# A two-block kernel: latent projections on unscaled rows, head scales spread by DMA, angles computed earlier

## The reference

```python
h = rmsnorm(x, norm_g)
proj = h @ w_in          # q_lat 384, kv_lat 256, k_pe 32, ...
q = (rmsnorm(q_lat, q_norm_g) @ w_uq).reshape(B, S, N_HEADS_MLA, QK_HEAD_DIM)
kv = (rmsnorm(kv_lat, kv_norm_g) @ w_ukv).reshape(B, S, N_HEADS_MLA, QK_NOPE_DIM + V_HEAD_DIM)
k_nope, v = split_cols(kv, (QK_NOPE_DIM, V_HEAD_DIM))
q = rope_tail(rmsnorm(q, q_head_g), cos, sin)
k = rope_tail(rmsnorm(k, k_head_g), cos, sin)
o_attn = blocked_bidirectional_attention(q, k, v) * jax.nn.silu(g_attn)
```

## Time and profile before

| | us |
|---|---|
| median of 3 runs | 2633.99 (2633.96 to 2637.42) |
| the profiled execution, its own time | 2636.41 |
| its span, first to last instruction | 2634.3 |
| PE busy in the span | 2507.5 (95%) |
| DVE, POOL, ACT busy | 1313.3, 873.7, 756.2 |
| from the last MLP matmul to the first matmul of lat | 1303.62 to 1324.52 |
| heads, first matmul to last sums | 1404.67 to 1499.31 |
| first scores of MLA | 1525.53 |

### The profile page before, as it was taken

One profiled execution on the slowest core, in us unless ns is written; L12 is line 12 of the kernel. 1 busy time (PEld: TensorE's weight loads), 2 busy tenths in 40 slices (PEclk: granted clock), 3 DMA queues, 4 the chain that ended last, 5 costly groups with the idle time before them and its releaser, 6 DMA issues.

```text
span 2634.3 us, 33963 instructions
## 1 busy us (share of the span) xinstructions
PE 2507.5 (95%) x13700; PEld 2048.6 (78%) x13700; DVE 1313.3 (50%) x1325; ACT 756.2 (29%) x1158; POOL 873.7 (33%) x383
## 2 busy tenths in 40 slices
PE   6999888899999999999899989999999999989999
PEld 3788677677888888888677678888888878878877
DVE  3799688636444445444575777741023221341341
ACT  4201277614111211111144367731000120241010
POOL 1444300043434444344333200024444434423442
PEclk8999899999999999999999999999999999999999
DMA  6111455211111111111211000011111111113112
GB/s 258 43 45 56 126 171 178 107 55 37 53 48 49 48 48 48 48 48 48 88 56 40 25 1 1 1 33 49 50 63 48 49 41 50 64 40 112 49 48 88
DMA packets 54965, 165.31 MB, mean 63 GB/s; under 512 B 5364, under 2 KB 23928, under 8 KB 53432
## 3 DMA queue, kind: packets, MB, share of 16 engines
q1 hardware_dynamic: 49152, 140.68, 16.2%
q10 hardware_dynamic: 5688, 22.81, 2.2%
HBM read 152.98 MB, written 10.49 MB: 62 GB/s over the span
## 4 chain that ended last, share of the span: by engine, by line
PE 85%; DVE 7%; ACT 3%; issue 2%; POOL 1%; DMA 1%; SPq 0%; DVEq 0%; ACTq 0%; POOLq 0%
PE region L275 25%; PE region L277 24%; PE region L276 24%; PE aux L1789 2%; PE pv L1799 2%; PE pv L369 1%; DVE conv L1139 1%; ACT na_prob L1023 1%; DMA x_sb<-x_t 1%; DVE na_prob L1064 1%; POOL w_hi L2211 1%; POOL w_lo L2214 1%; PE pv L833 1%; PE region L2083 1%; PE pv L983 1%
## 5 line engine op out<-in xcount | busy, mean ns | idle before, releaser
L2211 POOL TENSOR_TENSOR w_hi<-w_raw,der 128x1024 fp32r<-128x1024 f32 x186 | 363.5, 1954 | 1550.6 <-PE region L277 1522.2
L275 PE MATMUL region<-h_hi,w_hi 128*128 128x512 f32 x1760 | 692.2, 393 | 15.0 <-DVE h_lo L440 5.4
L276 PE MATMUL region<-h_lo,w_hi 128*128 128x512 f32 x1760 | 688.1, 391 | 0.0
L277 PE MATMUL region<-h_hi,w_lo 128*128 128x512 f32 x1760 | 687.8, 391 | 0.0
L2214 POOL TENSOR_TENSOR w_lo<-w_raw,w_hi 128x1024 fp32r<-128x1024 f32 x186 | 502.6, 2702 | 14.6
L275 PEld LDWEIGHTS region<-h_hi,w_hi 128*128 128x128 f32 x1760 | 332.4, 189 | 94.3 <-issue 11.9
L277 PEld LDWEIGHTS region<-h_hi,w_lo 128*128 128x128 f32 x1760 | 332.3, 189 | 70.2
L276 PEld LDWEIGHTS region<-h_lo,w_hi 128*128 128x128 f32 x1760 | 332.6, 189 | 68.0
L275 PE MATMUL region<-ff_hi,w_hi 128*128 128x512 f32 x512 | 199.2, 389 | 0.0
L276 PE MATMUL region<-ff_lo,w_hi 128*128 128x512 f32 x512 | 199.2, 389 | 0.0
L277 PE MATMUL region<-ff_hi,w_lo 128*128 128x512 f32 x512 | 199.2, 389 | 0.0
(11 more groups left out here) (351 smaller groups left out, 3764.0 us busy)
## 6 DMA issues: line engine op xcount, KB each, us to landing
w_raw<-units SPq DMA_DIRECT2D x186, 512.0 KB, 3.3
w_raw<-w_ada_late SPq DMA_DIRECT2D x32, 512.0 KB, 4.3
bias<-na_bias SPq DMA_DIRECT2D x24, 384.0 KB, 3.7
ada_buf<-w_ada SPq DMA_DIRECT2D x4, 2048.0 KB, 28.5
x_sb<-x_t ACTq DMA_DIRECT2D x2, 2048.0 KB, 13.7
v_pair<-v_spill SPq DMA_DIRECT2D x64, 64.0 KB, 3.4
x<-x_t ACTq DMA_DIRECT2D x1, 4096.0 KB, 14.8
x_spill<-x ACTq DMA_DIRECT2D x1, 4096.0 KB, 11.2
```

The lines of the kernel that those rows point to most:

```text
L275: pe.matmul(dst, wh, xh, start=first, stop=False)
L276: pe.matmul(dst, wh, xl, start=False, stop=False)
L277: return pe.matmul(dst, wl, xh, start=False, stop=last)
L2211: pool.tensor_tensor(w_hi[:, s], w_raw[:, s], one_col.broadcast_to([P, 1024]), ALU.mult)\
```

## The change

Five things are changed together, all between the MLP and MLA.

1. **Unscaled start of lat.** In the last MLP group ACT and DVE also split `x1` times the gain, without the norm's scale, into `h2_hi` and `h2_lo`. The first two lat units are projected from these; the nf sums stand among their blocks as the sixth, the spread as the eleventh. `n3_act` and `n3_dve` then overwrite the parts with scaled ones for units 3 to 6, each block once unit 2 has used it (`lat_free`), and DVE multiplies the first two results by the scale (`scale`).
2. **Angles earlier.** The angle steps (two for each of the 8 first units) and both sines run in the first MLP group, which is taken out of the loop, as the last is.
3. **Head scales.** `half_ones` packs a head's sums in 8 groups of 16 rows, so root and reciprocal work on 128 columns. PE spreads nothing: SP stores 8 rows of 128 to DRAM, waits for that, and loads the line into all 128 partitions of one of three SBUF tiles (`head_wide0` to `2`). `finish` is two heads late in place of one and reads that tile. The root of head h waits for the load of head h-2.
4. **SP's order.** Six unit loads stand between these pairs of DMAs.
5. **No meeting before MLA**; ACT rounds the first head among the copies of uv.

```diff
             for f in range(KD):
+                if first and f == 6:
+                    sine(0, sin2)
...
             for d in range(KD):
+                if first and d == 1:
+                    sine(1, cos2)
...
+                if last:
+                    e.activation(h2_hi[:, d], x1[:, d], ACT.Identity, scale=both_g[:, d:d + 1]).then_inc(sem("nu_hi"), 1)
+
+        group(0, True, False)
+        with e.Fori(1, FF_GROUPS - 1) as g:
+            group(g, False, False)
+        group(FF_GROUPS - 1, False, True)
...
                     low(f - 1)
+                if first:
+                    angle_dve(e, ch, 2 * f)
+                    angle_dve(e, ch, 2 * f + 1)
...
+                if last:
+                    reach(e, "nu_hi", d + 1)
+                    e.scalar_tensor_tensor(out=h2_lo[:, d], in0=x1[:, d], scalar=both_g[:, d:d + 1], in1=h2_hi[:, d].bitcast(F32),
+                                           op0=ALU.mult, op1=ALU.subtract).then_inc(sem("nu_lo"), 1)
...
-    def nf_pe(e, pos):
+    def nf_sums_pe(e):
         reach(e, "nf_acc", 14 * FF_GROUPS + 1)
         packed_sums(e, aux[:, 0:QTR], tmp[:, 2]).then_inc(sem("nf_sqmm"), 1)
         packed_sums(e, aux[:, HALF:HALF + QTR], tmp[:, 3]).then_inc(sem("nf_sqmm"), 1)
+
+    def nf_spread_pe(e):
         reach(e, "nf_rs", 1)
         spread(e, pv_flat, nf_b).then_inc(sem("nf_spread"), 1)
...
+    def n3_act(e, pos):
+        for k in range(KD):
+            t = tmp[:, k % 2]
+            reach(e, "n3_nm", k + 1)
+            e.activation(t, t, ACT.Identity, scale=both_g[:, k:k + 1]).then_inc(sem("n3_af"), 1)
+            reach(e, "n3_af", k + 1)
+            if k < KD - 1:
+                reach(e, "lat_free", k + 1)
+            else:
+                e.wait_ge(unit_done, UNIT0["lat"] + 2)
+            copy(e, h2_hi[:, k], t).then_inc(sem("n3_hi"), 1)
+            if k in (2, 3):
+                use = pos.next_use()
+                e.wait_ge(unit_done, UNIT0["lat"] + k - 1)
+                copy(e, q_lat[:, k - 2], region[:, use % 2]).then_inc(free[use % 2], 1)
+
+    def n3_dve(e, pos):
+        def low(k):
+            reach(e, "n3_hi", k + 1)
+            e.tensor_tensor(h2_lo[:, k], tmp[:, k % 2], h2_hi[:, k].bitcast(F32), ALU.subtract).then_inc(sem("n3_lo"), 1)
+
+        def scale(i):
+            use = pos.next_use()
+            e.wait_ge(free[use % 2], use // 2 + 1)
+            e.tensor_tensor(q_lat[:, i], q_lat[:, i], pv_flat, ALU.mult).then_inc(sem("lat_scaled"), 1)
+
+        for k in range(KD):
+            if k >= 2:
+                reach(e, "n3_lo", k - 1)
+            e.tensor_tensor(tmp[:, k % 2], x1[:, k], pv_flat, ALU.mult).then_inc(sem("n3_nm"), 1)
+            if k:
+                low(k - 1)
+        low(KD - 1)
+        scale(0)
+        scale(1)
+        reach(e, "n3_lo", KD)
...
-        start_pair(e, pos, UNIT0["lat"], h2_hi, h2_lo, lambda k: reach(e, "n3_lo", k + 1))
-        unit(2)
-        unit(3)
+        assert pos.use % 2 == 0 and UNIT0["lat"] % 2 == 0
+        for i, (n, k) in enumerate(LAGGED):
+            if i == 5:
+                nf_sums_pe(e)
+            if i == 10:
+                nf_spread_pe(e)
+            if k == 0:
+                e.wait_ge(unit_split, UNIT0["lat"] + n + 1)
+                wait_region(e, pos.use + n)
+            if n == 0:
+                reach(e, "nu_lo", k + 1)
+            w = slice(k * P, k * P + P)
+            for lo in (0, HALF):
+                last = mm3(e, region[:, n, lo:lo + HALF], w_hi[:, n, w], w_lo[:, n, w],
+                           h2_hi[:, k, lo:lo + HALF], h2_lo[:, k, lo:lo + HALF], k == 0, k == KD - 1)
+            if k == KD - 1:
+                last.then_inc(unit_done, 1)
+            elif n == 1:
+                last.then_inc(sem("lat_free"), 1)
+        pos.use += 2
+        start_pair(e, pos, UNIT0["lat"] + 2, h2_hi, h2_lo, lambda k: reach(e, "n3_lo", k + 1))
...
         for i in range(LATS):
-            use = pos.next_use()
-            e.wait_ge(unit_done, UNIT0["lat"] + i + 1)
             dst = q_lat[:, i] if i < NQL else kv_lat[:, i - NQL]
-            copy(e, dst, region[:, use % 2]).then_inc(free[use % 2], 1)
-            e.wait_ge(free[use % 2], use // 2 + 1)
+            if i < 2:
+                reach(e, "lat_scaled", i + 1)
+            else:
+                use = pos.next_use()
+                e.wait_ge(unit_done, UNIT0["lat"] + i + 1)
+                copy(e, dst, region[:, use % 2]).then_inc(free[use % 2], 1)
+                e.wait_ge(free[use % 2], use // 2 + 1)
...
-            if i < 2:
-                reach(e, "angle", i + 1)
-                e.activation((sin2, cos2)[i][RR], tmp[RR, 2], ACT.Sin).then_inc(sem("table"), 1)
...
-        reach(e, "pos_ld", 16)
-        ch(e.tensor_copy(tmp[r, 0], pos_i[r]))
-        ch(e.tensor_scalar(tmp[r, 0], tmp[r, 0], par[r, SMALL["invf"]:SMALL["invf"] + 1], None, ALU.mult))
...
-        for which, (quarter, shift) in enumerate([(0.0, 0.0), (0.25, np.pi / 2)]):
-            ch(e.tensor_scalar(tmp[r, 1], tmp[r, 0], 1.0 / TWO_PI, quarter, ALU.mult, ALU.add))
-            ch(e.tensor_scalar(tmp[r, 1], tmp[r, 1], magic, magic, ALU.add, ALU.subtract))
...
-            e.tensor_scalar(tmp[r, 2], tmp[r, 2], -3.1415925, None, ALU.max).then_inc(sem("angle"), 1)
-        reach(e, "angle", 2)
-        reach(e, "table", 1)
+        reach(e, "table", 2)
         ch(e.tensor_scalar(sin2[r], sin2[r], par[r, SMALL["sign"]:SMALL["sign"] + 1], None, ALU.mult))
-        reach(e, "table", 2)
         ch(e.memset(q_table[0:NOPE], 1.0))
         ch(e.tensor_copy(q_table[NOPE:QK], cos2[NOPE:QK]))
         ch(e.tensor_copy(q_table[QK:P], sin2[QK:P]))
+        ch(e.memset(half_ones[:], 0.0))
+        for a in range(2):
+            ch(e.memset(half_ones[:, a, 16 * a:16 * a + 16], 1.0))
...
+        def __init__(self, tag, heads, scale, wide=None):
+            self.tag, self.heads, self.scale_at, self.wide = tag, heads, scale, wide
+
+        def spread_sp(self, e, h):
+            reach(e, f"{self.tag}_rs", h + 1)
+            if h >= 3:
+                reach(e, f"{self.tag}_sc", h - 2)
+            line = v_spill[0, 8 * h:8 * h + 8]
+            e.dma_start(line, self.scale_at[0:P:16, h % 2, 0:P]).then_inc(sem("wide_st"), 16)
+            reach(e, "wide_st", 16 * (h + 1))
+            e.dma_start(self.wide[h % 3][:], line.rearrange("a c -> (a c)").partition_broadcast(P)).then_inc(sem(f"wide_ld{h % 2}"), 16)
+
+        def reach_wide(self, e, h):
+            reach(e, f"wide_ld{h % 2}", 16 * (h // 2 + 1))
 
...
+                    for a in range(2):
+                        for q in range(4):
+                            at = (2 * q + a) * P
+                            last = e.matmul(aux[32 * q:32 * q + 32, bank:bank + P], half_ones[0:rows, a], src[:, at:at + P],
+                                            start=(a == 0), stop=(a == 1))
+                elif self.heads[h].packed:
                     last = packed_sums(e, aux[:, bank:bank + QTR], src, rows)
                 else:
...
-                if h >= 2:
+                if h >= 2 and not self.wide:
                     spread_scale(h - 2)
             n = len(self.heads)
             sums(n - 1)
-            spread_scale(n - 2)
+            if not self.wide:
+                spread_scale(n - 2)
             if meanwhile:
                 meanwhile()
-            spread_scale(n - 1)
+            if not self.wide:
+                spread_scale(n - 1)
 
...
                 reach(e, f"{tag}_ss", h + 1)
                 if h >= 2:
-                    if self.heads[h - 2].packed:
+                    if self.wide:
+                        self.reach_wide(e, h - 2)
+                    elif self.heads[h - 2].packed:
                         reach(e, f"{tag}_spread", sum(x.packed for x in self.heads[:h - 1]))
                     else:
                         reach(e, f"{tag}_sc", h - 1)
                 bank = (h % 2) * HALF
-                root_act(e, tag, self.scale_at[:, h % 2], aux[:, bank:bank + QTR], self.heads[h].rows, eps_col)
+                n = P if self.wide else QTR
+                root_act(e, tag, self.scale_at[:, h % 2, 0:n], aux[:, bank:bank + n], self.heads[h].rows, eps_col)
 
             for h, head in enumerate(self.heads):
                 use = pos.next_use()
...
+                if self.wide:
+                    self.reach_wide(e, h)
+                elif packed:
                     reach(e, f"{tag}_spread", sum(x.packed for x in self.heads[:h + 1]))
-                rs = pv_flat if packed else self.scale_at[:, h % 2]
+                rs = self.wide[h % 3] if self.wide else pv_flat if packed else self.scale_at[:, h % 2]
                 self.heads[h].finish(e, ch, self.heads[h].dst, rs)
                 e.sem_inc(sem(f"{tag}_sc"), 1)
 
+            late = 2 if self.wide else 1
             for h in range(len(self.heads)):
                 pos.next_use()
-                inverse_dve(e, tag, h + 1, self.scale_at[:, h % 2])
```

(41 more changed lines are left out.)

70 lines of the change are left out of this document (47 added, 23 removed).

## The result

| kernel | median us | runs | against before, 95% interval | span of the profiled run | mean clock |
|---|---|---|---|---|---|
| before | 2634.77 | 2633.96 to 2637.42 | | 2634.3 | |
| after | 2597.89 | 2597.12 to 2600.76 | 0.986 (0.9843 to 0.9877) | 2595.3 | 0.986 |

The change gives 36.9 us by the medians and 39.0 by the spans. The forecast was 44, to 2590, in a range of 2576 to 2606. The start of lat gave 2.5 us more than its term and the heads gave 6.4 us less, so the total came out nearer than its terms. The two stretches of the traces give 17.5 + 22.6 = 40.1 us; the spans have 39.0, because after reached the MLP 0.7 us later and took 0.4 us more behind the first scores.

The account below looks back on a forecast made before the run. PE was taken to bound the heads before the change, DVE's queue beside POOL's splits after it. Part A's 15 us and part B's 29 make 44, from the median 2634.0 to 2590 us; range 2576 to 2606.

Parts of the forecast that it names:

- Part A: Unscaled start of lat behind the MLP: 19.2 us gained at most, less 4 of stall, so 15 us (11 to 19).
- Waits, slow start and spread: PE behind the MLP: three waits of 14.9 us, slow restart 2.4, spread 1.9 would go, together 19.2 us.
- The stall: In lat, PE waits for scaled blocks whose remainders DVE makes late beside POOL's splits: 4 us, 0 and 8 as ends.
- third rival: Lat: scaled blocks come 8 us or more late, ACT copying two results between them; part A gives 4, 2601 us; chance 0.08.
- The collisions: Lat: each of two POOL splits catches about 1.1 of DVE's remainders, 2.2 us each, 5 us late after two.
- The rival of a moved wait: Lat: the unscaled start moves the wait instead of removing it, blocks 8 us or more late; 2601 us, chance 0.08.
- Angles and extra roundings: Moved into the MLP's first group and added in its last, hidden by DVE's idle time: nothing either way.
- Part B: Heads, from their start to the first scores: 120.9 us becomes 92, a gain of 29 us (20 to 39).
- DVE's work: Heads: 5 heads at 5.9 us, 3 at 4.7 and 8 at 4.4, together 79 us.
- the charge for POOL: Heads: 2 us of DVE time for each POOL split, on every second q head and every third k head.
- The round trip: Heads' scales: store 2.0, load 3.3, issue and semaphores 0.8 us; hidden under DVE's 4.4 a head until the last head.
- The slow rival: Heads: the broadcast load takes 17 us, part B 171 us, 50 lost and 15 won, 2669 us; chance 0.05.

Follow-up runs that it names:

- unscaled_alone: The unscaled start of lat and the earlier angles alone, with the heads as in before: 2619.12 us, 0.9938 of before.
- copy_early: after with ACT's two copies of the unscaled first lat results out of PSUM one position earlier in ACT's order: 2595.50 us, 0.9845 of before.
- turn_early: after with DVE's five operations that turn the keys' rotary rows put beside heads 0 and 1 instead of 1 to 5: 2594.03 us, 0.9833 of before.
- turn_after_store: after with the edits of turn_early and root_after_store together: 2593.71 us, 0.9842 of before.
- root_after_store: after with ACT's root of head h waiting for the store of head h-2's scales, not their load: 2597.87 us, 0.9858 of before.
- two_stores: after with each head's scales stored twice, one after the other, to lengthen each round trip: 2612.27 us, 0.9901 of before.

## Why the prediction was right, and where it was off

**Part A, 15 us (11 to 19), was 17.5** (100.66 to 83.14; 18.1 in unscaled_alone). Waits, slow start and spread went as summed: PE goes on without a gap and the clock stays at 1.00 up to the third product. The stall was taken at 4 us and came to about that, 2.25 of gap and 1.7 by eight matmuls at the lower clock behind it; that the number fits is luck. Its cause was another: PE was held by ACT's copy out of PSUM, which the prediction named only in its third rival, and not by the remainders. copy_early showed that the remainders are next in line, with 2.58 us. The collisions were lighter than charged: 2.2 us had been put on each of 2.2 remainders, 4.8 in sum; four were caught (2.26, 2.17, 1.66, 2.17 against 1.22 us), for 0.4 to 1.0 us each, 3.4 in sum. What made the gain larger is that the sums, which were to stay at 1.9 us, took 1.07, and that two waits of 0.40 and 0.34 us later in lat are gone; some 0.7 us stay open. The rival of a moved wait (8 us) did not come. Angles and extra roundings cost nothing, as forecast: the first group of the MLP takes 176.8 us in after and in before, the last 174.2 in both.

**Part B, 29 us (20 to 39), was 22.6** (120.9 to 98.3; 21.0 with both at the slow start, so that 1.6 us of it are the luck of one execution). The mechanism was that of the forecast: DVE's queue and POOL beside it. The terms against the trace:
- DVE's work was put at 79 us. From the heads' start it was 3 reciprocals and one rotation before 1408.5, 3.6 us, and 75.0 us from there to the end of the last finishing (1483.52), with 1.26 of waiting for the last load in it: 77.3 of work. Right, and with it the charge for POOL (12.8 us, where 5 x 1.0, 3 x 1.0 and 8 x 0.7, 13.6 us, had been put on the heads). But "`finish` read PSUM" held for one of its two operations on q only: the multiplication by `q_table` had both inputs in SBUF already, and the rotation too, and they carry 7.0 of the 12.8.
- The start was the failed step: "DVE starts when head 1 is projected and head 0 summed, some 11 us in". Only the reciprocals start there. Finishing 0 stands in DVE's order behind reciprocal 2, since finishing is two heads late now. It started 20.7 us in (1408.55), while its load had landed some 4 us before. DVE had 3.6 us of work until then instead of 9.7: 6.1 us lost on a queue that is full from there on.
- The tail was put at 2.4 us and took 2.6. So 20.7 + 75.0 + 2.6 = 98.3, where 11 + 79 + 2.4 = 92 had been forecast, and the start is nearly the whole of the difference: 20.7 - 11 - 3.6 = 6.1. Of after's start the quick first head took off 1.6 us; in copy_early, with the slow one, finishing 0 starts 22.3 us in.
- The instructions' order, which was known, held this before the run. The sum used DVE's total work with a start time, and not the place of the first long operation in the queue. turn_early and turn_after_store, which put other work into that hole, bear it out with 4.7 and 4.9 us; a kernel that finishes one head late with these loads was not run.

**The round trip**, 6.1 us taken, took 5.1 to 6.5 from a reciprocal's end to what its load releases, median 5.8 over the eleven that were waited for (store to load 1.65 as a rule, load 3.3 to 4.3, median 3.8). The Trainium skill, "DMA: Bandwidth & Descriptors", § Anatomy of one DMA, gives its 2.0 us and 436 GB/s for DMAs that GpSimd issues, and these are issued by SyncE, which the prediction passed over. By it the trip was 5.2 us as an estimate; the runs put the median at 0.6 more. "Under DVE's 4.4, so it is hidden until the last head" holds for after (root_after_store), with little room (two_stores). The slow rival, 17 us for a broadcast load, is out. "SP's six unit loads, nothing" is a bit off. A load issued shortly ahead of a store draws the step from store to load out:

```profile
1441.95 0.32 SPq L1728 DMA_DIRECT2D head_wide<-v_spill  x1
1443.69 0.57 SPq L1726 DMA_DIRECT2D v_spill<-head_scale  x1
1446.04 0.32 SPq L1728 DMA_DIRECT2D head_wide<-v_spill  x1
...
1472.83 0.43 SPq L2282 DMA_DIRECT2D w_raw<-units  x1
1474.49 0.57 SPq L1726 DMA_DIRECT2D v_spill<-head_scale  x1
1477.39 0.32 SPq L1728 DMA_DIRECT2D head_wide<-v_spill  x1
```

2.35 us behind a load of scales, where DVE's queue hides it; 2.90 behind the last unit load, and that is the last trip, for which DVE then waits 1.26 us.

**What the prediction didn't have as a term**: the meeting and the copies of values, 5.3 us, which it counted within part B without a price.

## What to carry to other kernels

When a scale is applied one head later to hide a transfer, the engine that applies it has less to do at the start and the same to do in all; on a full queue, what it didn't do at the start comes back at the end (6.1 us here), so give it the side work in that hole (4.7 us won back). A wait that the profile puts down to a DMA may belong to the engine that feeds the DMA: take the transfer out of the wait and see whether the wait stays. And moving an operand out of PSUM to save an engine's turn makes the reader a neighbour of POOL; count the splits that fall beside it, and beside the operations that had both inputs in SBUF before, since a new order moves them too. Last, two lengths cut from a trace tell more than a median where the edits are worth less than the scatter ahead of the place they touch.

## What the runs showed of the hardware

- In the heads, a DVE operation of 1024 columns with both inputs in SBUF took 1.22 to 1.29 us alone and up to 3.3 beside a POOL split; with the splits cut to 16 columns none was over 1.29. It isn't slowed but held: all 13 such operations of after from 1320 us on that started during a split ended 1.07 to 1.09 us behind the split's end, whether they took 1.66 us or 3.29. It works the other way round as well: at 1454.94 the operation came just ahead of the split and took 1.22 us, and the split took 2.92 in place of 1.89.
- An operation with the second input in PSUM wasn't held: those on `x1` and `pv` took 1.22 us inside a split (1327.20, 1330.55, 1333.38 in after). An operation with one tensor input wasn't always spared: the first of the rotation (TENSOR_SCALAR, 64 rows) took 0.75 us alone and 2.68 beside a split in turn_early; the reciprocals of 128 columns took 0.95 us everywhere, three of those of after wholly inside a split. By the same section of the Trainium skill ("VectorE: DVE Perf Modes", § Two Vector instructions with no wait between them), an instruction with one tensor input reads it through the shared interface when it runs in a mode that uses both ports. The two kinds of rows would agree with it if the reciprocal runs in no such mode, which no run here shows.
- A reciprocal took 0.95 us on 128 columns and 1.75 on 256, so 0.80 for 128 columns more.
- A store of 4 KB (8 rows of 512 bytes) was seen complete by its queue 1.65 to 1.76 us after its issue in 13 of 16 cases. The other three took 1.94, 2.35 and 2.90; a load of 512 KB had been issued 2.7, 1.7 and 1.7 us before them.
- The same first nine microseconds of the heads, behind the same wait of 2.5 us, ran at a granted clock of 1.00 in three of the traces and of about 0.81 in the other eleven, 1.6 us apart; behind the gap of 2.25 us in lat it fell in after and stayed up in root_after_store. What decides it, no run here shows.
